# B's transposed rows by a transposing transfer, block two's bias rows by one product

## The reference, cut to what matters

```python
# block one, SSD, per layer: x, B, C after a causal convolution and silu
states = jnp.einsum("bclgn,bclgep->bcgepn", bc, x * decay_states[..., None])   # B of chunk 0 is needed with tokens on rows
cb = jnp.einsum("bclgn,bcsgn->bgcls", cc, bc)

# block two, attention in a block: one bias for each distance and head
s_own = (jnp.einsum('bhqd,bhkd->bhqk', qc, kown)
         + bias_h[:, t5_bucket(jnp.maximum(dist_own, 0))][None])
```

## Time and profile before

| | us |
|---|---|
| median of three runs | 1522.9 |
| profiled execution, device time | 1522.75 |
| its span | 1520.9 |
| PE busy | 1511.7 (99%) |
| DVE busy | 1039.8 (68%) |
| ACT busy | 926.7 (61%) |
| POOL busy | 182.1 (12%) |

### The profile page before, as it was taken

How to read it: one execution, slowest core, us unless ns; L and a number is a source line. 1 busy time by engine, 2 the same in 40 slices (tenths; PEclk the granted TensorE clock), 3 DMA queues, 4 the chain that set the end, 5 groups by cost and what they waited for, 6 DMA issues and landing times.

```text
span 1520.9 us, 19048 instructions
## 1 busy us (share of the span) xinstructions
PE 1511.7 (99%) x7644; PEld 1278.7 (84%) x7644; DVE 1039.8 (68%) x1326; ACT 926.7 (61%) x1119; POOL 182.1 (12%) x115
## 2 busy tenths in 40 slices
PE   9999999999999999999999999999999999999998
PEld 9888888888888888988888888888888888888887
DVE  6978876756665554888886776665545676677665
ACT  6776786574365553757777565436555555666564
POOL 2001121422000100001102332100010020002000
PEclk9999999999999999999999999999999999999999
DMA  8455666875457674555557685437757584447541
GB/s 297 168 159 168 193 193 189 206 210 165 171 204 217 191 236 172 186 153 189 170 178 203 184 228 184 164 139 244 221 171 250 214 259 163 150 152 242 175 152 65
DMA packets 132400, 288.10 MB, mean 189 GB/s; under 512 B 97079, under 2 KB 98008, under 8 KB 101848
## 3 DMA queue, kind: packets, MB, share of 16 engines
q1 hardware_dynamic: 131208, 284.44, 58.6%
q10 hardware_dynamic: 1104, 2.43, 0.5%
HBM read 261.69 MB, written 1.84 MB: 173 GB/s over the span
## 4 chain that ended last, share of the span: by engine, by line
PE 93%; DVE 5%; ACT 1%; issue 1%; DMA 0%; SPq 0%; ACTq 0%; DVEq 0%
PE ps L678 25%; PE ps L680 25%; PE ps L679 25%; PE ps L683 2%; PE ps L931 2%; PE ps L932 2%; PE ps L933 2%; DVE w_low L1712 2%; PE ps L802 2%; PE ps L817 1%; DVE conv L1798 1%; PE ps L819 1%; ACT w_high L1187 1%; PE ps L789 0%; PE ps L807 0%
## 5 line engine op out<-in xcount | busy, mean ns | idle before, releaser
L1712 DVE TENSOR_TENSOR w_low<-w_raw,w_high 128x2048 fp32r<-128x2048 f32 (+2 forms) x251 | 575.1, 2292 | 369.1 <-ACT w_high L1187 301.8
L678 PE MATMUL ps<-w_high,u_high 128*128 128x512 f32 x1376 | 547.4, 398 | 0.5 <-DVE w_low L1712 0.5
L680 PE MATMUL ps<-w_high,u_low 128*128 128x512 f32 x1376 | 536.8, 390 | 0.0
L679 PE MATMUL ps<-w_low,u_high 128*128 128x512 f32 x1376 | 536.0, 390 | 0.0
L1187 ACT ACTIVATE w_high<-w_raw 128x2048 fp32r<-128x2048 f32 (+1 forms) x196 | 369.2, 1884 | 259.3 <-PE ps L680 245.3
L678 PEld LDWEIGHTS ps<-w_high,u_high 128*128 128x128 f32 x1376 | 258.5, 188 | 55.4 <-issue 2.4
L680 PEld LDWEIGHTS ps<-w_high,u_low 128*128 128x128 f32 x1376 | 258.2, 188 | 55.0
L679 PEld LDWEIGHTS ps<-w_low,u_high 128*128 128x128 f32 x1376 | 258.7, 188 | 53.9 <-issue 2.4
L678 PE MATMUL ps<-w_high,b_high 128*128 128x512 f32 x384 | 151.6, 395 | 0.0
L680 PE MATMUL ps<-w_high,b_low 128*128 128x512 f32 x384 | 149.7, 390 | 0.0
L679 PE MATMUL ps<-w_low,b_high 128*128 128x512 f32 x384 | 149.5, 389 | 0.0
(11 more groups left out here) (244 smaller groups left out, 1524.6 us busy)
## 6 DMA issues: line engine op xcount, KB each, us to landing
w_raw<-in_stream SPq DMA_DIRECT2D x238, 1024.0 KB, 4.9
w_raw<-in_stream SPq DMA_DIRECT2D x12, 512.0 KB, 4.1
par<-in_pars SPq DMA_DIRECT2D x4, 269.0 KB, 5.8
h<-in_x SPq DMA_DIRECT2D x4, 256.0 KB, 5.1
ple_gain<-in_ple_g ACTq DMA_DIRECT2D x2, 512.0 KB, 5.0
out<-h SPq DMA_DIRECT2D x4, 256.0 KB, 2.0
scratch<-in_const SPq DMA_DIRECT2D x1, 768.0 KB, 7.2
rev<-scratch ACTq DMA_DIRECT2D x1, 768.0 KB, 4.1
```

Of the source, the lines that this page charges most:

```text
L678: nc.tensor.matmul(o, hi, whi, start=start, stop=False, **kw)
L679: nc.tensor.matmul(o, hi, wlo, start=False, stop=False, **kw)
L680: return nc.tensor.matmul(o, lo, whi, start=False, stop=stop, **kw)
L1712: return nc.vector.tensor_tensor(out=o, in0=a, in1=b, op=op)
```

## The change

In block one, B's four turns on PE and ACT's copy go. POOL, after the mask rows, waits for B's silu and copies B's chunk 0 (128 x 512 floats) with its 16-bit halves apart; SP waits for that copy right after it has issued the load of chunk 9 and issues one transposing transfer of 128 x 1024 halves; POOL waits for it and puts the halves together in `btok`. This is done in both layers. In block two the four products become one with four stationary columns, so that four partitions hold the four bias rows; ACT copies 4 x 384 floats once, and the store to HBM writes the same 128 rows from these four partitions, with a repeated source.

```diff
+        b_half = words("b_halves", Q_AT, [2, GROUPS, P])[:, :, :, :]
+        b_back = words("b_turned", Q_AT + 512, [2 * GROUPS, P])[:, :, :]
...
-        rev_rows = X[:, at[0] + 512:at[0] + 512 + 4 * REV].rearrange("p (h j) -> p h j", h=4)
+        rev_rows = X[0:4, at[0] + 512:at[0] + 512 + REV]
...
+                    if c == 9:
+                        sp.wait_ge(rows_masked.sem, rows_masked.at(l, 2))
+                        sp.dma_start_transpose(b_back, b_half.rearrange("p h g n -> p (h g n)")).then_inc(b_turned.sem, 16)
...
-                    for g in range(GROUPS):
-                        last = turn(ps[:, 4, tok(g)], BC[:, g, tok(0)])
-                    last.then_inc(bc_ps.sem, 1)
...
-                    last.then_inc(bc_ps.sem, 1)
+                    last.then_inc(step_ps.sem, 1)
...
-                    for hh in range(4):
-                        last = nc.tensor.matmul(ps[:, 4 + hh, 0:REV], rev_in[:, REV + hh:REV + hh + 1].to_broadcast([BUCKETS + 1, P]),
-                                                rev_in[:, 0:REV], start=True, stop=True)
-                    last.then_inc(rev_ps, 1)
+                    nc.tensor.matmul(ps[0:4, 4, 0:REV], rev_in[:, REV:REV + 4], rev_in[:, 0:REV], start=True, stop=True)\
+                        .then_inc(rev_ps, 1)
...
-                    if c == 10:
-                        act.wait_ge(bc_ps.sem, bc_ps.at(l, 1))
-                        nc.scalar.activation(btok, four(ps[:, 4, :]), ACT.Copy).then_inc(btok_out.sem, 1)
...
-                        for b in range(2):
-                            ins = nc.scalar.activation(rev_rows[:, 2 * b:2 * b + 2, :], ps[:, 4 + 2 * b:6 + 2 * b, 0:REV], ACT.Copy)
-                        ins.then_inc(rev_out, 1)
+                        nc.scalar.activation(rev_rows, ps[0:4, 4, 0:REV], ACT.Copy).then_inc(rev_out, 1)
                         act.wait_ge(rev_out, 1)
-                        act.dma_start(rev, rev_rows.rearrange("p h j -> p (h j)")).then_inc(rev_stored, 16)
+                        act.dma_start(rev.rearrange("p (h j) -> h p j", h=4), rev_rows.unsqueeze(1).to_broadcast([4, P, REV])).then_inc(rev_stored, 16)
...
+                pool.wait_ge(conv_act.sem, conv_act.at(l, 1))
+                nc.gpsimd.tensor_copy(b_half, BC[:, 0:4, tok(0)].bitcast(U16).rearrange("p g (n h) -> p h g n", h=2)).then_inc(rows_masked.sem, 1)
+                pool.wait_ge(b_turned.sem, b_turned.at(l, 16))
+                nc.gpsimd.tensor_copy(btok.bitcast(U16).rearrange("p g (n h) -> p h g n", h=2),
+                                      b_back.rearrange("p (h g) n -> p h g n", h=2)).then_inc(btok_out.sem, 1)
...
-                        dve.wait_ge(bc_ps.sem, bc_ps.at(l, 2))
+                        dve.wait_ge(step_ps.sem, step_ps.at(l, 6))
```

More of the change, by code:

```diff
@@ L370, in build @@
         ffn_cols = signal("ffn_cols", 4)
-        step_ps = signal("step_ps", 5)
-        bc_ps = signal("bc_ps", 2)
+        step_ps = signal("step_ps", 6)
+        b_turned = signal("b_turned", 16)
         xt_ps = signal("xt_ps", GROUPS)
@@ L454, in build @@
         act_rows = signal("act_rows", NGU)
-        rows_masked = signal("rows_masked", 1)
+        rows_masked = signal("rows_masked", 2)
         rows_loaded = [signal(f"rows_loaded{t}", 16 * GROUPS) for t in range(T)]
```

## The result

The changed kernel takes 1539.83 us (median of 4 runs, 1539.12 to 1540.75); the kernel before, run beside it, 1523.68 us (1522.6 to 1524.5). The ratio is 1.011, 95% interval 1.0095 to 1.0124: slower by 16 us, where +12.6 us (1535.4 us) was forecast, inside the range of 1520.3 to 1548. (The median of before sits between two groups of times, on which experiments 8 and 9 have more.)

The account below looks back on a forecast made before the run. PE was taken to bound the kernel nearly everywhere, with DVE setting the end from 42.9 to 60.1 us of each layer. -0.9 + 4.4 - 2.1 + 11.2 = +12.6 us on 1522.75 gave 1535.4 us, range 1520.3 to 1548.

Parts of the forecast that it names:

- B's turns, -0.43 us a layer: Block one, PE before c = 9: removing B's four turns saves 0.43 us a layer, 0.9 us in two.
- Rival 3: Block one: B's transfer lands so late that PE's c = 9 waits, some 5 us a layer at 27 us; chance 0.03.
- POOL's first copy holds DVE 1.0 us: Block one, 42.8 to 43.9 us: POOL's copy meets DVE's small steps at 42.89 us, which lose 1.0 us.
- POOL's second copy, 1.2 us between 0 and 1.4: Block one, from about 50 us: POOL's 1.4 us copy back meets DVE's convolution steps, costing 1.2 us, between 0 and 1.4.
- Rival 2: The store is fast and POOL's copies cost DVE nothing: -3.0 us, 1519.8 us, 0.2% faster; chance 0.19.
- The product, -2.1 us: Block two, c = 3: one bias product of 0.69 us replaces four of 2.77 us, gaining 2.1 us.
- The store, 31 us: Block two: the bias store from four partitions, at one sixteenth's rate of 27 GB/s, lands 31 us after issue, at 1256.0 us.
- rival 1: The store is fast, under 19.9 us, and POOL delays DVE as forecast: +1.4 us, 1524.2 us, no change; chance 0.25.
- the budget of 19.9 us: Block two: the store may take 19.9 us at no cost, since ACT must be let go by 1244.8 us.
- The path: Block two: ACT's wait for the store at c = 8 holds its later work; PE, before c = 10, waits 11.2 us.

Follow-up runs that it names:

- experiment 8: Kernel 1 with ten useless 128 x 128 products on PE ahead of its wait for the decays; 1525.32 us, ratio 1.0018 to the kernel before.
- experiment 9: The kernel before with its four bias products made twice, eight in all; 1528.33 us against 1522.63, ratio 1.0032.
- kernel 6: Kernel before plus block one's edits, with POOL's first copy after x0's convolution, the transfer and PE's wait for B's rows later; 1522.09 us, ratio 0.9996.
- kernel 1: The kernel before with only block one's edits (B turned by POOL copies and a transposing transfer); 1527.14 us against 1522.62, ratio 1.003.
- experiment 3: The kernel before, only its bias store reading four neighbouring partitions (0 to 3), each repeated 32 times in 6 KB runs; 1539.84 us, one run.
- experiment 4: The kernel before, only its bias store reading four spaced partitions (0, 4, 8, 12), each repeated 32 times in 6 KB runs; 1524.23 us, one run.
- experiment 2: The kernel before with only block two's edits (one product, one copy, store from four partitions); 1537.94 us, ratio 1.0099.

## Why the prediction was right, and where it was off

The sign, the places and the mechanism in the main were right, and 12.6 us of 16 to 18 were counted. Step by step:

- *B's turns, -0.43 us a layer.* Right: PE's first product of the next stage follows the turn of the decays without them, and PE never waits for B's rows. Rival 3, the late transfer, is out: B's rows are there at 51.87 us, against 51.4 forecast.
- *POOL's first copy holds DVE 1.0 us.* Measured 0.74 us: the small step started 0.14 us into the copy and had its own 0.24 us to do anyway, which the sum had forgotten. The prediction's rule, that a DVE step begun inside a POOL copy waits for its end, came out: the step ended 0.08 us behind the copy.
- *POOL's second copy, 1.2 us between 0 and 1.4.* Measured 1.03 us of a copy of 1.35 us. The Trainium skill, "SBUF — State Buffer", "Who interferes with whom", is borne out in its kind (a convolution step with two SBUF inputs is held by a copy that reads SBUF); the row is 0.3 us below its full length. By kernel 6 it goes both ways: POOL's copy of 1.04 us took 3.03 us when DVE came first. Rival 2, in which DVE loses nothing, is out. In all 1.74 us a layer in place of 2.2.
- *The product, -2.1 us.* Measured -2.0 us. What the step did not see is that four products can cost more than their own length: in some executions the clock is halved behind them (experiments 8 and 9).
- *The store, 31 us.* Measured 35.7 us. It is the term mis-sized most. The rate was taken as one sixteenth of 430 GB/s; the rows show 22 to 25 GB/s. The Trainium skill's 27.6 GB/s for partitions 0 to 3 ("SBUF — State Buffer", "Door 1: The DMA port swizzle") gives 28.5 us for the bytes, an estimate; with nothing else on top this case has 786 KB / 35.7 us = 22 GB/s, the same kind of limit and a fifth less. That the place of the four partitions makes the difference is shown by experiments 3 and 4; one way out shared by neighbours is what fits it. Why it runs below the page's figure is not shown: weight loads write into the same four partitions at the same time, which was not varied.
- *The rule behind rival 1* (the Trainium skill, "DMA: Bandwidth & Descriptors", "Why a DMA increments its semaphore by 16 and not by 1": the outermost dimension sets the number of engines, four here) does not decide this case. Experiments 3 and 4 both have a source of four and differ by 15.6 us. The shares of the store's queue, 21.3% and 19.0% of 16 engines, in the first window of each, are 3.4 and 3.0 engines at work, which agrees with four in both; what these engines moved differs threefold.
- *What is queued behind, and the budget of 19.9 us.* Right: a store of 13.7 us at most (experiment 4) costs nothing, one of 35.7 us does. By the budget 35.7 us give 35.7 - 19.9 = 15.8 us, and with the 2.0 us of the product the start of c = 10 should be 13.8 us later than block one's 4.0 us alone would make it, which is what was measured. ACT needed 13.7 us behind the store, 13.5 us forecast.
- *The path.* That the wait for the store ended last is partly luck. The text had named shared DMA engines only as a reason for a longer store, and did not see that the store would delay the weight loads (13 to 18 us in place of 4.9) and the transposing transfers (24.3 in place of 5.9 us). PE's first wait, 2.47 us, is theirs, and in experiments 2 and 3 so is the end of the chain. In the changed kernel the second transposing transfer, issued at 1262.83 us, landed 12.0 us later, 0.8 us before its merging copies began; so without any wait on `rev_stored` PE's c = 10 would have started less than 1 us earlier, an estimate from these times that no run tested.
- *PE's clock.* Not in the sum at all. In layer 0 it cost 1.5 us. In block two it was at half for a while too, but there PE had to wait for ACT, and the chain does not go through it.
- *Why the forecast was low.* Of the 5.5 us between 12.6 and 18.1 us, 4.6 are the store's (15.8 in place of 11.2 us), 0.5 block one's (a clock that was left out, against a loss of DVE and POOL that was taken too high), 0.1 the product's, and 0.3 us, behind L1063, are not attributed.

The terms as measured: block one -0.9 + 3.5 + 1.5 = +4.1 us (seen at block two's start: +4.0), block two -2.0 + 15.8 = +13.8 us (seen at c = 10: +13.8; to the end of the span: +14.1).

## What to carry to other kernels

Bytes to be sent out by DMA should lie on many partitions, and few ones must be spaced: four neighbours made a store of 35.7 us where four spaced partitions took 13.7 us at most and 128 took 4.1, and it slowed the weight loads and transposing transfers beside it, which cost nearly as much as the wait for the store itself. A copy on GpSimd is free only where VectorE has slack, since in the overlaps seen here either held the other for most of the copy; put it behind the stretch in which VectorE is waited for. Where TensorE itself sets the end, count a new wait of it at more than its length, as in layer 0, and test a repair by keeping the engine at work through it.

## What the runs showed of the hardware

- Behind idle times of 2.22 us (changed kernel) and 2.16 us (kernel 1) in layer 0 TensorE's granted clock was 0.50 (1.2 GHz) for 3 us; behind 2.16 and 2.30 us in layer 1 of the same two kernels it stayed at 1.00. With ten useless products in the idle time of layer 0 it was at 1.00 (experiment 8). Behind 2.47 us in block two it was 0.50 for 3 us; in the wait of 7.98 us it fell near 1263.5 us, with TensorE still idle, and came back at 1273.6 us.
- The clock also falls with TensorE never idle: behind four products of 33 rows and 384 columns in the profiles of kernels 4 and 8, not in that of before, and for ten microseconds with eight of them. It fits the two groups of times, 1522.5 and 1524.3 us, of the kernel before.
- A store bounded by one group of neighbouring partitions took loads of 1 MB from 4.9 to 13 to 18 us and a transposing transfer from 5.9 to 24.3 us. Between 1256 and 1264 us, with the store, weights and that transfer under way, the DMA engines moved 39 GB/s in all at a busy share of 1.24.
- A store of 786 KB read from four partitions, four apart, ran at up to 72 GB/s; from four neighbours at 24.
